# Where the small vector work of a long one-core kernel stands: constants, a running sum, four multiplies and the rest of the mean in six norms

## What is computed

```python
def layer_norm(x, g, b):
    mu = jnp.mean(xf, axis=-1, keepdims=True)
    xc = xf - mu
    var = jnp.mean(xc * xc, axis=-1, keepdims=True)
    y = xc * lax.rsqrt(var + LN_EPS) * g + b
```

## Time and profile before

| | us |
|---|---|
| median of 3 runs | 1865.61 |
| lowest and highest | 1859.04, 1868.11 |
| profiled execution | 1870.4 |
| its span, first to last instruction | 1868.6 |
| TensorE busy | 1827.5 (98%) |
| VectorE busy | 1268.5 (68%) |
| ScalarE busy | 1165.7 (62%) |
| GpSimd busy | 418.8 (22%) |
| mean granted TensorE clock | 0.991 |

### The profile page before, as it was taken

How to read it: one execution, slowest core, us unless ns; L and a number is a source line. 1 busy time by engine, 2 the same in 40 slices (tenths; PEclk the granted TensorE clock), 3 DMA queues, 4 the chain that set the end, 5 groups by cost and what they waited for, 6 DMA issues and landing times.

```text
span 1868.6 us, 32954 instructions
## 1 busy us (share of the span) xinstructions
PE 1827.5 (98%) x11306; PEld 1608.9 (86%) x11306; DVE 1268.5 (68%) x1916; ACT 1165.7 (62%) x1905; POOL 418.8 (22%) x448
## 2 busy tenths in 40 slices
PE   9999999999999999999999999999999999999998
PEld 8778888898698888888889988889888888788887
DVE  7887776764776766666667866666666565667665
ACT  5476565643655746588548778744687454758853
POOL 4003320230533302021122032211021120632112
PEclk9999999999999999999999999999999999999999
DMA  7525366576353565565635546654656546026662
GB/s 247 173 69 169 114 202 191 182 194 184 108 169 102 192 189 186 177 193 189 216 116 172 186 133 194 204 179 147 187 185 203 201 130 198 35 91 201 184 220 70
DMA packets 87340, 312.11 MB, mean 167 GB/s; under 512 B 10432, under 2 KB 15680, under 8 KB 86976
## 3 DMA queue, kind: packets, MB, share of 16 engines
q1 hardware_dynamic: 86944, 309.01, 53.1%
q10 hardware_dynamic: 288, 1.64, 0.3%
HBM read 309.56 MB, written 1.05 MB: 166 GB/s over the span
## 4 chain that ended last, share of the span: by engine, by line
PE 88%; DVE 5%; ACT 3%; issue 2%; POOL 2%; DMA 0%; SPq 0%; POOLq 0%; ACTq 0%; DVEq 0%
PE pt L520 42%; PE pt L521 21%; PE pt L514 5%; PE pt L515 4%; PE pt L516 4%; PE pt L636 1%; DVE w_lo L1919 1%; PE pt L640 1%; PE pt L638 1%; PE pt L1178 1%; PE pt L959 1%; ACT w_hi L1289 1%; PE pt L1081 0%; POOL spare L2757 0%; PE pt L677 0%
## 5 line engine op out<-in xcount | busy, mean ns | idle before, releaser
L1919 DVE TENSOR_TENSOR w_lo<-raw,w_hi 128x1024 fp32r<-128x1024 f32 (+2 forms) x546 | 705.4, 1293 | 279.3 <-ACT w_hi L1289 271.2
L1289 ACT ACTIVATE w_hi<-raw 128x1024 fp32r<-128x1024 f32 (+2 forms) x546 | 597.6, 1096 | 384.3 <-PE pt L521 223.6
L520 PE MATMUL pt<-in_both,w_hi 128*128 128x512 f32 x2103 | 743.3, 398 | 0.6 <-DVE in_both L2550 0.5
L521 PE MATMUL pt<-in_both,w_lo 128*128 128x256 f32 x2103 | 590.4, 281 | 0.0
L520 PEld LDWEIGHTS pt<-in_both,w_hi 128*128 128x128 f32 x2103 | 395.6, 188 | 98.6 <-DVE w_lo L1919 1.4
L520 PE MATMUL pt<-act_both,w_hi 128*128 128x512 f32 x1309 | 463.9, 399 | 0.0
L521 PEld LDWEIGHTS pt<-in_both,w_lo 128*128 128x128 f32 x2103 | 397.8, 189 | 0.1
L521 PE MATMUL pt<-act_both,w_lo 128*128 128x256 f32 x1309 | 366.7, 280 | 0.0
L520 PEld LDWEIGHTS pt<-act_both,w_hi 128*128 128x128 f32 x1309 | 245.7, 188 | 60.8 <-issue 1.5
L521 PEld LDWEIGHTS pt<-act_both,w_lo 128*128 128x128 f32 x1309 | 247.1, 189 | 0.2
L2722 POOL TENSOR_TENSOR act_both<-scr,act_both 128x256 f32 x88 | 100.3, 1139 | 498.4 <-ACT act_both L1806 498.4
(11 more groups left out here) (341 smaller groups left out, 2337.9 us busy)
## 6 DMA issues: line engine op xcount, KB each, us to landing
raw<-in_fi SPq DMA_DIRECT2D x176, 512.0 KB, 3.6
raw<-in_ff SPq DMA_DIRECT2D x128, 512.0 KB, 3.6
raw<-in_fo SPq DMA_DIRECT2D x64, 704.0 KB, 4.1
raw<-in_dq SPq DMA_DIRECT2D x24, 512.0 KB, 3.7
raw<-in_mq SPq DMA_DIRECT2D x16, 512.0 KB, 4.0
raw<-in_mo SPq DMA_DIRECT2D x16, 512.0 KB, 3.9
raw<-in_rg_u SPq DMA_DIRECT2D x10, 512.0 KB, 3.7
raw<-in_rg_y SPq DMA_DIRECT2D x10, 512.0 KB, 3.6
```

What stands on the lines that cost most here:

```text
L520: nc.tensor.matmul(pt[:, b, :], lhs_hi, both.rearrange("p t s -> p (t s)"), start=start, stop=False)
L521: return nc.tensor.matmul(pt[:, b, 0:S], lhs_lo, both[:, 0, :], start=False, stop=stop)
L1289: nc.scalar.activation(w_hi[:, u.slot(), w], raw[:, u.slot(), w], ACT.Copy).then_inc(hi_split, 1)
L1919: v.tensor_tensor(w_lo[:, u.slot(), w], raw[:, u.slot(), w], w_hi[:, u.slot(), w].bitcast(F32), ALU.subtract).then_inc(lo_split, 1)
```

## The change

In the first stage only the scaling of `mq0` stays. The other small instructions move behind the units 0 to 4 of `na_k`, and ScalarE waits for `const_ready` 3 ahead of the gates. `warm`, a dummy target, gets another column, since the softplus' numbers now live longer.

In `rg`, the multiply of the pairs 0, 2, 3 and 4 moves to GpSimd, behind its last `conv_lo`; the scan waits for `scan_input`.

In norm 4, VectorE makes the running sum of the first four chunks itself, in `into_y_centred`.

In all norms, LN_EPS is subtracted from the squared rest of the mean (so it is added to the variance), VectorE takes the reciprocal of the variance, and ScalarE the root of that; TensorE waits for `ln_root` and spreads the root. In norms 0 to 4 VectorE subtracts the rest of the mean from all eight chunks, chunk k + 1 just ahead of the scaling of chunk k; bank 6, ScalarE's copy and GpSimd's subtractions are gone. In norm 5 they stay, but bank 6 is filled behind bank 4.

```diff
@@ pe, into_layer_norm
                 pe.wait_ge(rest_cols, n + 1)
                 broadcast_columns(7, ln_rest).then_inc(rest_wide, 1)
-                broadcast_columns(6, ln_rest).then_inc(rest_wide, 1)
-                pe.wait_ge(ln_inverse, n + 1)
+                pe.wait_ge(ln_root, n + 1)
                 broadcast_columns(4, ln_rs).then_inc(rstd_wide, 1)
+                if n == 5:
+                    broadcast_columns(6, ln_rest).then_inc(rest_wide, 1)
@@ act, layer_norm
-                act.wait_ge(var_done, n + 1)
-                nc.scalar.activation(ln_rs, ln_var, ACT.Sqrt, bias=lneps).then_inc(ln_root, 1)
-                act.wait_ge(rest_wide, 2 * n + 2)
-                nc.scalar.activation(ln_rest_wide, pt[:, 6, 0:S], ACT.Copy).then_inc(rest_copied, 1)
+                act.wait_ge(ln_inverse, n + 1)
+                nc.scalar.activation(ln_rs, ln_var, ACT.Sqrt).then_inc(ln_root, 1)
+                if last:
+                    act.wait_ge(rest_wide, n + 2)
+                    nc.scalar.activation(ln_rest_wide, pt[:, 6, 0:S], ACT.Copy).then_inc(rest_copied, 1)
@@ act, ahead of gates
+            act.wait_ge(const_ready, 3)
@@ dve, mem_k_after
                 if m.base == 6:
-                    gains_scaled()
-                    softplus_begun()
+                    v.tensor_scalar(gain("mq0", 0, 4), gain("mq0", 0, 4), 1.0 / 16, None, ALU.mult
+                                    ).then_inc(const_ready, 1)
             units("mem_k", after=mem_k_after)
             columns("mt", 1)
-            softplus_series()
-            decays()
@@ dve, na_k
-            units("na_k", after=scaled_to(big, 8, None))
+            na_keys = scaled_to(big, 8, None)
+
+            def na_k_after(m):
+                na_keys(m)
+                if m.base == 0:
+                    gains_scaled()
+                if m.base == 1:
+                    softplus_begun()
+                if m.base == 2:
+                    softplus_series((17, 15, 13, 11))
+                if m.base == 3:
+                    softplus_series((9, 7, 5, 3))
+                if m.base == 4:
+                    decays()
+            units("na_k", after=na_k_after)
@@ dve, into_y_centred
+                    if sums and 0 < b < FIRST_MEAN:
+                        dve.wait_ge(acc_free, LN_ACC[n] + b + 1)
+                        if b > 1:
+                            dve.wait_ge(first_sum, (FIRST_MEAN - 1) * n + b - 1)
+                        v.tensor_tensor(mean_sum, y[:, 0, :] if b == 1 else mean_sum, y[:, b, :], ALU.add
+                                        ).then_inc(first_sum, 1)
@@ dve, layer_norm
                 link(v.tensor_tensor(ln_restsq, ln_rest, ln_rest, ALU.mult))
+                link(v.tensor_scalar(ln_restsq, ln_restsq, LN_EPS, None, ALU.subtract))
                 dve.wait_ge(var_ready, n + 1)
                 v.scalar_tensor_tensor(out=ln_var, in0=pt[:, 4:6, 0], scalar=1.0 / D, in1=ln_restsq,
                                        op0=ALU.mult, op1=ALU.subtract).then_inc(var_done, 1)
-                dve.wait_ge(rest_wide, 2 * n + 1)
-                for k in range(DVE_RECENTRE):
-                    if k == 1:
-                        dve.wait_ge(ln_root, n + 1)
-                        v.reciprocal(ln_rs, ln_rs).then_inc(ln_inverse, 1)
-                    e = v.tensor_tensor(y[:, k, :], y[:, k, :], pt[:, 7, 0:S], ALU.subtract)
-                link(e)
+                dve.wait_ge(var_done, n + 1)
+                v.reciprocal(ln_var, ln_var).then_inc(ln_inverse, 1)
+
+                def recentre(k):
+                    return v.tensor_tensor(y[:, k, :], y[:, k, :], pt[:, 7, 0:S], ALU.subtract)
+                dve.wait_ge(rest_wide, n + 1)
+                recentre(0)
+                link(recentre(1))
                 dve.wait_ge(rstd_wide, n + 1)
                 for k in range(DC + 2):
+                    if 1 <= k < (DVE_RECENTRE if last else DC) - 1:
+                        link(recentre(k + 1))
                     if k < DC:
-                        if k >= DVE_RECENTRE:
-                            dve.wait_ge(recentred, (DC - DVE_RECENTRE) * n + k - DVE_RECENTRE + 1)
+                        if last and k >= DVE_RECENTRE:
+                            dve.wait_ge(recentred, k - DVE_RECENTRE + 1)
@@ dve, scan
-                v.tensor_tensor(st, st, chunks(big, 2 * p, 2), ALU.mult)
+                if p == 1:
+                    v.tensor_tensor(st, st, chunks(big, 2 * p, 2), ALU.mult)
+                else:
+                    dve.wait_ge(scan_input, (0, 2, 3, 4).index(p) + 1)
@@ pool, norm_sums(n, first) and behind conv_lo
-                for k in range(1, FIRST_MEAN):
+                for k in range(1, FIRST_MEAN) if first else ():
-                pool.wait_ge(rest_copied, n + 1)
+                if n < 5:
+                    return
+                pool.wait_ge(rest_copied, 1)
+            for p in (0, 2, 3, 4):
+                st = chunks(big, 20 + 2 * p, 2)
+                pool.wait_ge(lru_root, p + 1)
+                pool.wait_ge(gated_wide, p + 1)
+                g_.tensor_tensor(st, st, chunks(big, 2 * p, 2), ALU.mult).then_inc(scan_input, 1)
```

17 lines of the change are left out of this document (9 added, 8 removed).

## The result

| | before | after |
|---|---|---|
| median, us (21 runs each) | 1865.64 | 1872.74 |
| lowest and highest | 1859.04, 1873.70 | 1867.27, 1881.55 |
| ratio, 95% interval | | 1.0043 [1.0031, 1.0056] |
| profiled span, us | 1868.6 | 1874.1 |
| mean granted TensorE clock of the span | 0.991 | 0.986 |

The change costs 7.1 us where 3.9 us of gain were forecast; 1872.7 lies above the range's 1868.5. The sign of the sum was wrong, and one term of it, the norms, is why.

What follows compares the result with a forecast made beforehand. TensorE, busy almost always, was taken as the bound, through its waits and clock. First stage −5.5, multiplies −1.6, running sum −0.3, norms +2.9, last norm +0.6 sum to −3.9 us: 1865.6 to 1861.7 us, range 1855 to 1868.5.

Steps and rivals of the forecast that it cites:

- The norms, +2.9: Norms 0 to 4: VectorE's extra subtractions make TensorE wait for low parts, +1.3 × 2 + 0.1 × 3 = +2.9 us.
- for the mix of the profiled execution: Norms 0 to 4: the +2.9 us counts two norms with the clock up and three with it down.
- then just part 1 is late: Norms at 1.2 GHz: TensorE wants chunks each 1.92 us, only low part 1 is late, +0.1 us a norm.
- The root's path, −0.21 a norm: Norms: reciprocal ahead of the root, nothing after it, so the broadcast starts earlier, −0.21 us a norm.
- The first stage, −5.5: Memory stage: constants' arithmetic moved out, TensorE starts in_t earlier (−3.2) and its clock stays up (−2.3), −5.5 us.
- 4.4 − 1.2: Start of in_t: TensorE's wait at L514 falls from 4.4 to 1.2 us, giving −3.2 us.
- 4.5 us at half rate: Behind the start of in_t: the half-rate stretch from 64.2 to 68.7 us shrinks by 2.25, giving −2.3 us.
- The multiplies, −1.6: Recurrent stage: four multiplies to GpSimd erase 1.8 us of TensorE's waits, less 0.2 net for contention, −1.6 us.
- the multiplies block VectorE in full: Rival, recurrent stage: three operations × 1.3 us exceed 2.5, so no gain there; 1863.3 us, chance 0.1.
- The running sum in `do`, −0.3: Norm after do: sum on VectorE starts TensorE 0.9 us earlier, mostly given back at GpSimd's squares, −0.3 us.
- Norm 5, +0.6: Last norm: GpSimd's subtractions start later because their broadcast follows the root's, +0.6 us.
- The slower one: Rival: VectorE bounds every norm, +6.5 us with the clock up in all five; 1869.2 us, chance 0.08.

Runs made afterwards that it cites:

- norms_filled: Kernel before with the new norms, plus four broadcasts that nobody reads to keep TensorE busy in norms 0 to 4; 1872.55 us, ratio 1.0031.
- after_again: The changed kernel, unaltered, run once more for a second profile; 1875.22 us, one execution.
- norms: Kernel before with the whole change of the norms and nothing else; 1875.18 us, ratio 1.0048.
- recentre_only: Kernel before with VectorE alone subtracting in norms 0 to 4, bank 6's broadcast gone there, root and reciprocal as before; 1877.83 us, ratio 1.0061.
- norms_skip: Kernel before with the new norms, but nobody subtracts the rest of the mean from chunks 3 to 7 in norms 0 to 4; 1868.99 us, ratio 1.0003.
- root_only: Kernel before with only the reciprocal put ahead of the root and the root spread, subtractions as before; 1866.20 us, ratio 1.0000.
- moves: The changed kernel with the norms of before, so all the change outside the norms; 1863.39 us, ratio 0.9985 against before.
- moves_root_filled: Kernel before with all moves outside the norms, reciprocal ahead of the root, old subtractions, two unread broadcasts in norms 0 to 4; 1862.58 us, ratio 0.9982.
- skip_bank6: norms_skip with TensorE again broadcasting into bank 6, unread, ahead of the root's broadcast in norms 0 to 4; 1865.22 us, ratio 0.9989 against before.
- before_again: The kernel before, unaltered, run once more for a second profile; 1858.11 us, one execution.

## Why the prediction was wrong, point by point

**The norms, +2.9: the step that failed; measured +7.1 in the profiled pair, 9.2 by the run of the norms alone.** VectorE's pace was as forecast, and its size with the clock up was right: chunks 1.24 us apart, +1.2 us a norm (norms_filled), +1.3 forecast. What failed is the sentence "for the mix of the profiled execution": I multiplied by two norms with the clock up and three with it down, as if the change left that alone. It didn't. Norms 1 and 4, up before, fell, and took +2.9 and +3.1 us; norms 0, 2 and 3, down in both, took +0.1, +0.6 and +0.4 where +0.1 each was forecast. The term for a norm with the clock down, "then just part 1 is late", +0.1, was too small as well: 0.36 on average in this pair, and 0.7 by norms against norms_skip. The sum says nothing of the removed broadcast into bank 6; I never asked what its absence does to TensorE's clock. And the profile of before is one draw: 8 falls in 25 norms over five profiles with the old norm, 20 in 20 with VectorE alone subtracting and no filler (after, after_again, norms, recentre_only).

**The root's path, −0.21 a norm: right to the first product, worth nothing behind it.** GpSimd's subtractions hold up the first low part by as much as it starts earlier (root_only). In the new norm there is no GpSimd, but VectorE's pace decides.

**The first stage, −5.5: measured −1.3 in the pair and about −2.2 over sixteen profiles.** What would come late next was right: in after, ScalarE's first high part starts 0.12 us behind the last product of `mem_v` and TensorE 1.24 us behind it, and the clock from 58 to 65 us is 1.00. In `na_k` the arithmetic cost nothing, as forecast: TensorE's waits from 425 to 530 us are the same in both profiles.

```profile
63.75 0.51 ACT L1310 ACTIVATE in_both<-x,par 128x256 fp32r<-128x256 f32 x1 [1.32 <-PE pt L641]
...
64.87 0.36 PE L515 MATMUL pt<-in_both,w_hi 128*128 128x256 f32 x1 [1.24 <-issue]
...
58.00:65.00 7.00, 5.76 (x26) 4.46 (x25) 5.67 (x8) 3.54 (x7) 0.00 (x0) 1.00 0.49 157
```

But TensorE started `in_t` at 64.87, not at 61.0. It had lost 2.48 us near 22 us to GpSimd's sum over the memory tokens (0.67 in the profile of before, the same code), and the clock with it for 3.4 us. With the old code part of such a loss is made up at `in_t`: the wait there was 4.42 us when the early one was 0.67 (before), and 1.92 when that was 2.25 (recentre_only). The nine profiles without the move say so less neatly: the wait at `in_t` was 3.9 us on average in the three with an early wait of 0.7, 3.1 in the three with 1.4 to 1.5, 2.5 in the three with 2.2 to 2.3. The stretch at 0.50 behind it was 6.8 us long in two of the nine, 3.4 in six, and absent in one. The forecast of 4.4 − 1.2, and that of 4.5 us at half rate, were taken from an execution in which TensorE was early and the stretch was the long one. Also, in three of the seven profiles with the move (moves, after_again, moves_root_filled) the clock fell for 3.4 us from 83 to 85 us on instead, during or behind a row of 20 small products (32 columns each in moves). None of the nine without the move had it at that place but norms_skip, at 87.3.

**The multiplies, −1.6: measured −0.53.** The queue's arithmetic was right: with the multiplies gone TensorE gains 1.66, and I had 1.75 at the products. The term that failed is the contention, which I took as 0.2 net; two VectorE instructions took 1.85 us more, 1.15 of it net of ScalarE's slack (16.44 − 15.29). The row that I had, L2505 with 0.96 instead of 0.47, said twice the duration or nearly so for an instruction that meets GpSimd; I had it in hand and chose the low end. That is nearly the rival "the multiplies block VectorE in full", which counted three meetings of 1.3 us; there were two, of 0.94 and 0.91. On the place of the gain I was wrong as well: no wait on VectorE's weights at `rg_out` was to be left, and it stayed 1.29 us, since VectorE's chain from `lru_product` on moves as a whole.

The Trainium skill (SBUF — State Buffer, section Who interferes with whom) lets the two instructions exclude each other. The two meetings in this trace agree: the three instructions of each end one after another, about 1.1 us apart, and both sides pay (VectorE +0.94 and +0.91 us, GpSimd 2.33 and 2.23 us for a multiply that alone took 1.3). That the part still gave 0.53 and not 0 is no evidence against the rule. The first two multiplies ran while VectorE waited for ScalarE and met nothing.

**The running sum in `do`, −0.3: about −0.1.** L1098's wait fell by 1.0 and L1082's rose by 0.9, both as forecast to 0.2 us. In after GpSimd's squares ran without a gap from 1658.18:

```profile
1658.18 4.23 POOL L2811 TENSOR_TENSOR spare<-spare 128x256 f32<-128x256 f32 x3 [18.91 <-ACT spare L1753]
```

**Norm 5, +0.6: right.** From the column sums to the span's end it took 10.57 us before and 11.20 after. GpSimd starts 1.0 us later against them (0.9 forecast), and its work is as long as in the earlier trace rows:

```profile
1867.23 3.47 POOL L2825 TENSOR_TENSOR y<-y,scr 128x256 f32<-128x256 f32 x5 [9.59 <-ACT scr L1773]
...
1867.58 4.54 SPq L507 DMA_DIRECT2D out<-x  x8
```

**The rivals.** The slower one (VectorE the bound of every norm, 1869.2, chance 0.08) was the nearest: right in sign, and right that the other gains are smaller too. That its 6.5 us for the norms is near the measured 7.1 is luck in part: it wanted the clock up in all five, and it was down in all five. The parts as measured in the pair give 1865.6 − 1.3 − 0.5 − 0.1 + 7.1 + 0.6 = 1871.4, near the measured 1872.7. The range left out this rival of the prediction's own: 1869.2 lies above 1868.5. "Within 0.5%" is where the ratio's estimate lies, with the interval's upper end just beyond; the range was too narrow on the slow side.

## What to carry to other kernels

Work that TensorE does while it waits anyway is not a cost to be saved: count its idle time around a gap before and after an edit, and if some executions already show the lower clock there, price the edit with the clock down everywhere. A gain read from one execution's wait counts only against an engine that is equally early in the others. When small work moves to GpSimd beside VectorE, price each meeting of two such instructions as one behind the other (here +0.9 us on 1.23), and place the work where VectorE waits.

## What the runs showed of the hardware

- *Half a microsecond of products that nobody reads decided over the clock behind it in one pair of kernels.* With 0.45 us more of TensorE work ahead of the root's broadcast the clock fell in none of five norms, without it in five of five, for 3.4 to 6.8 us each (skip_bank6, norms_skip). The old norm has that broadcast and fell in 8 of 25 norms, in root_only in 4 of 5.
- *Vector work on two SBUF inputs and a GpSimd multiply went by turns.* Split, multiply, scan ended at 1029.3, 1030.5 and 1031.6 us, and scan, multiply, split at 1038.5, 1039.6 and 1040.7 (after); the one that began first kept its 1.2 us.
- *Products in a dense stretch have two paces, at one and the same clock.* Windows of before, then of before_again, in the same stretch of code, TensorE busy throughout, clock 1.00 in both:

```profile
700.00:750.00 50.00, 50.00 (x285) 43.39 (x284) 34.61 (x50) 32.91 (x60) 10.69 (x14) 1.00 0.59 188
```

```profile
700.00:750.00 50.00, 50.00 (x291) 44.10 (x290) 35.16 (x51) 32.68 (x59) 10.62 (x14) 1.00 0.60 191
```

A pair of one wide and one narrow product (L520, L521) starts each 353.3 ns in the first and each 346.7 ns in the second, by the mean of the starts, and a stretch of 10 to 300 us holds one of the two. Which one it has differs between executions of the same kernel. 160 us at the one instead of the other are 3 us, so it may be a large part of why the runs of one kernel spread over 9 to 15 us; that wasn't tested. What sets the pace wasn't found.
